# Weight loads, a norm block and four squares moved within the first phases of a fused three-layer block

## What is computed

```python
def gated_deltanet_mixer(h, w_in, conv_w, a_log, dt_bias, norm_w, w_out):
    proj = h @ w_in
    qkv, z, b_logit, a_logit = jnp.split(proj, [...], axis=-1)
    qkv = jax.nn.silu(causal_depthwise_conv(qkv, conv_w))
    q, k, v = jnp.split(qkv, [GDN_QK, 2 * GDN_QK], axis=-1)
    q, k = l2_normalize(q ...), l2_normalize(k ...)
    beta = jax.nn.sigmoid(b_logit)
    g = -jnp.exp(a_log) * jax.nn.softplus(a_logit + dt_bias)
    o = chunked_gated_delta_rule(q, k, v, g, beta)
    o = rms_norm(o, norm_w) * jax.nn.silu(z)
    return o @ w_out
```

## Time and profile before

| | us |
|---|---|
| median of 3 runs | 924.78 |
| lowest, highest | 924.2, 925.02 |
| the profiled execution | 924.2 |
| span of the profiled execution, first to last instruction | 922.2 |
| TensorE busy in it | 880.4 (95%) |
| VectorE busy | 693.7 (75%) |
| ScalarE busy | 509.7 (55%) |
| mean granted clock of TensorE | 0.974 of 2.4 GHz |

### The profile page before, as it was taken

The page is one execution under the profiler, slowest core; times in us unless marked ns, Lnnn a source line. Parts: engine busy times, 40 slices in busy tenths (PEclk is TensorE's granted clock), DMA queues, the critical chain, the costliest instruction groups (busy, mean ns, idle before and its releaser), DMA issues.

```text
span 922.2 us, 16363 instructions
## 1 busy us (share of the span) xinstructions
PE 880.4 (95%) x6434; PEld 820.2 (89%) x6434; DVE 693.7 (75%) x1116; ACT 509.7 (55%) x728; POOL 46.0 (5%) x48
## 2 busy tenths in 40 slices
PE   5899999989897999999999999999999989999997
PEld 5899998779776999999997899999887779999995
DVE  5677888945756777777758578899998789955874
ACT  5597877546445555555545564333345566445642
POOL 0001110122010000000000000000001220001000
PEclk9999999979998999999999979999999999999999
DMA  8735664620465477777776616555454445555441
GB/s 253 229 93 176 210 177 148 168 57 2 159 203 185 138 250 250 251 250 250 250 266 229 215 60 206 162 188 184 152 183 138 136 138 183 184 183 170 137 150 47
DMA packets 139476, 161.58 MB, mean 175 GB/s; under 512 B 17156, under 2 KB 112284, under 8 KB 139420
## 3 DMA queue, kind: packets, MB, share of 16 engines
q1 hardware_dynamic: 139419, 160.80, 53.6%
HBM read 156.58 MB, written 4.21 MB: 174 GB/s over the span
## 4 chain that ended last, share of the span: by engine, by line
PE 72%; DVE 15%; ACT 7%; issue 2%; DMA 2%; SPq 0%; DVEq 0%; ACTq 0%
PE psum L480 22%; PE psum L482 21%; PE psum L481 21%; DVE w_lo L1376 5%; PE psum L765 3%; DVE cv L1819 2%; ACT w_hi L933 2%; DMA w_raw<-in_sc_w_out_dram 1%; DVE Tq L1604 1%; DVE outer L1602 1%; DVE cacc L1525 1%; PE psum L635 1%; ACT junk L966 1%; DMA x<-in_x_dram 1%; PE psum L869 1%
## 5 line engine op out<-in xcount | busy, mean ns | idle before, releaser
L1376 DVE TENSOR_TENSOR w_lo<-w_raw,w_hi 128x1024 fp32r<-128x1024 f32 x264 | 321.0, 1239 | 139.2 <-ACT w_hi L933 138.1
L933 ACT ACTIVATE w_hi<-w_raw 128x1024 fp32r<-128x1024 f32 x264 | 274.1, 1057 | 213.2 <-PE psum L482 168.2
L480 PE MATMUL psum<-hT_hi,w_hi 128*128 128x256 f32 x1216 | 350.2, 288 | 6.3 <-DVE w_lo L1376 5.6
L481 PE MATMUL psum<-hT_lo,w_hi 128*128 128x256 f32 x1216 | 347.2, 286 | 0.0
L482 PE MATMUL psum<-hT_hi,w_lo 128*128 128x256 f32 x1216 | 347.2, 286 | 0.0
L480 PEld LDWEIGHTS psum<-hT_hi,w_hi 128*128 128x128 f32 x1216 | 236.9, 195 | 7.6 <-issue 4.4
L481 PEld LDWEIGHTS psum<-hT_lo,w_hi 128*128 128x128 f32 x1216 | 236.9, 195 | 0.3 <-issue 0.2
L482 PEld LDWEIGHTS psum<-hT_hi,w_lo 128*128 128x128 f32 x1216 | 236.6, 195 | 0.0
L1819 DVE SCALAR_TENSOR_TENSOR cv<-aP,par,cv 128x256 f32<-128x256 f32 x240 | 98.4, 477 | 0.0
L480 PE MATMUL psum<-w_hi,hT_hi 128*128 128x512 f32 x224 | 91.6, 409 | 4.1 <-DVE w_lo L1376 4.1
L482 PE MATMUL psum<-w_hi,hT_lo 128*128 128x512 f32 x224 | 87.5, 390 | 0.0
(11 more groups left out here) (283 smaller groups left out, 1059.1 us busy)
## 6 DMA issues: line engine op xcount, KB each, us to landing
w_raw<-in_w_in_dram SPq DMA_DIRECT2D x44, 1024.0 KB, 5.1
w_raw<-in_sc_w_in_dram SPq DMA_DIRECT2D x32, 1024.0 KB, 7.5
w_raw<-in_gdn_w_in_dram SPq DMA_DIRECT2D x24, 1024.0 KB, 5.5
ada<-in_w_ada_dram SPq DMA_DIRECT2D x24, 512.0 KB, 5.1
w_raw<-in_gdn_w_out_dram SPq DMA_DIRECT2D x8, 1024.0 KB, 5.3
w_raw<-in_sc_w_out_dram SPq DMA_DIRECT2D x8, 1024.0 KB, 7.5
w_raw<-in_w_ret_out_dram SPq DMA_DIRECT2D x8, 1024.0 KB, 4.9
w_raw<-in_w_conv_out_dram SPq DMA_DIRECT2D x4, 1024.0 KB, 4.9
```

The source lines that it names most:

```text
L480: pe.matmul(o, l_hi, r_hi, start=start, stop=False, skip_group_check=True)
L481: pe.matmul(o, l_hi, r_lo, start=False, stop=False, skip_group_check=True)
L933: act.activation(w_hi[j % 2 * 2 + h][:, :, :], raw[slot][:, h * KH2:(h + 1) * KH2, :], ACT.Copy).then_inc(hi_ready, 1)
L1376: return dve.tensor_tensor(o, whole, hi.bitcast(F32), ALU.subtract)
```

## The change

It has three parts. On SyncE, the loads of chunks 2 and 3 go behind the loads of `ba_raw` and the 14 small loads. On ScalarE, squares 4 and 5 leave the end of the qkv phase, and squares 4 to 7 stand in chunks 0 to 3 of z (before: 6 and 7 in chunks 0 and 1). On VectorE, the block of `bgt`, `ngk` and `wdec` at chunk 6 goes behind the two splits of its chunk, and its first wait asks for 1 of the two transposes instead of 2.

```diff
             chunk(0, 0, qkv_cols(0), wait=False)
             chunk(1, 1, qkv_cols(1), wait=False)
-            chunk(2, 2, qkv_cols(2), wait=False)
             ba0 = GQKV + GV
...
-            chunk(3, 3, qkv_cols(3), wait=False)
...
-            for g in range(RING, FIRST["gdn_out"]):
-                if g < FIRST["z"]:
+            for g in range(2, FIRST["gdn_out"]):
+                if g < 4:
+                    chunk(g, g, qkv_cols(g), wait=False)
+                elif g < FIRST["z"]:
                     chunk(g, g % RING, qkv_cols(g))
...
-            squares(4)
-            squares(5)
             silu(COUNT["qkv"] - 1)
 
             def beside_z(i, j, done):
                 c = 4 * i + j
-                if c < 2:
-                    squares(6 + c)
+                if c < 4:
+                    squares(4 + c)
...
             for c in range(COUNT["qkv"]):
-                if c == 6:
-                    dve.wait_ge(bg_turned, 2)
-                    dve.tensor_copy(bgt[:, :, :], bank(6, P)[:, 0:NT, :]).then_inc(bgt_ready, 1)
...
                 split_lo(0, 0, c + 1, 1)
                 split_lo(0, 0, c + 2, 0)
...
+                if c == 6:
+                    dve.wait_ge(bg_turned, 1)
+                    dve.tensor_copy(bgt[:, :, :], bank(6, P)[:, 0:NT, :]).then_inc(bgt_ready, 1)
+                    dve.wait_ge(bgt_ready, 1)
+                    dve.wait_ge(lnss_ready, 1)
...
```

More of the change, by code:

```diff
@@ L1580, in _ @@
                     dve.tensor_copy(par[:, 1:4, :].rearrange("p a n -> p (a n)")[:, 0:376], psum[:, 5, 0:376]).then_inc(small_ready, 1)
+                if c == 6:
[3 more added lines that the diff above has]
+                    dve.wait_ge(lnss_ready, 1)
+                    for t in range(NT):
+                        i = dve.scalar_tensor_tensor(out=twos(ngk[:, t, :]), in0=over(lnss[:, t, :], P, 2), scalar=-0.5,
+                                                     in1=twos(bgt[:, t, gr]), op0=ALU.mult, op1=ALU.subtract)
+                    i.then_inc(ngk_ready, 1)
+                    dve.wait_ge(ngk_ready, 1)
+                    dve.wait_ge(bg_turned, 2)
+                    dve.tensor_tensor(wdec[:, :], psum[:, 6, SEQ:SEQ + VH], ngk[:, 0, :], ALU.add).then_inc(wd_sub, 1)
                 if c in (8, 10, 12, 14):
```

## The result

| us | before | after |
|---|---|---|
| median | 924.33 (5 runs, 923.28 to 925.02) | 933.32 (5 runs, 931.78 to 934.69) |
| the profiled execution | 924.2 | 932.75 |
| its span | 922.2 | 930.7 |
| mean granted clock in it | 0.974 | 0.967 |

The ratio is 1.0098 with an interval from 1.0084 to 1.0111: 9.0 us slower, where 5.0 were forecast and the range ended at 932.4. Slower was right, the size was not.

A forecast was written before the change was run, and what follows sets the result against it. TensorE was taken as the bound. A 0, C 2.3, B 1.1 and one clock fall 1.6 made 5.0 us, added to the 924.78 us median for 929.8 us, with a range from 927.4 to 932.4.

The forecast's parts named there:

- Part A: SyncE's queue at the start: chunk 2 lands at about 23 us, early enough for TensorE, so the cost is 0.
- small-transfer rule: Start loads: transfers under 64 KB are descriptor-dominated; 14 small loads would take 9.5 us and cost TensorE about 3.4 us.
- Part C: VectorE at chunk 6: L635 waits 2.7 us for the moved block instead of 0.4, costing 2.3 us.
- Part B: ScalarE at the turn to z: L622 waits 2.9 us for square 4, less 1.8 of slack, net 1.1 us.
- The slack: z phase: TensorE's two waits for weight splits at 170 and 178 us fall away, giving back 1.8 us.
- The clock: Behind the two new waits: one fall to 1.2 GHz for 3.4 us, costing 1.6 us; chance 0.36.
- B's bounds: Cost at the turn to z: 0.6 us if a square comes earlier, 2.9 if VectorE's splits are held up.
- the case without a fall: Behind the two new waits the clock stays up, giving 928.2 us; chance 0.22.
- Rival 2: Both new waits, at L635 and L622, end in a clock fall, giving 931.4 us; chance 0.25.
- Rival 3: At the start chunk 2 lands after 25.5 us: up to 3.4 us more, 930 to 934 us; chance 0.06.
- rival 4: At the start x lands sooner, winning up to 1.9 us: 926.3 us (same, chance 0.06) or 922.9 (faster, 0.02).

The follow-up runs named there:

- A alone: Only the loads of chunks 2 and 3 moved behind the small loads, on the kernel before: median 925.38 us, ratio 0.9999 (0.9983 to 1.0015).
- With the filler: Kernel before with only the VectorE block moved, plus 20 useless matmuls ahead of L635: median 927.45 us, ratio 1.0034 (1.0016 to 1.0052).
- the run with its filler: Kernel before with only the squares moved, plus 21 useless matmuls ahead of L622: median 924.69 us, ratio 1.0000 (0.9985 to 1.0016).
- the whole change with the clock kept up: Changed kernel with useless matmuls in its two new waits, at L635 and L622: median 927.46 us, mean 927.40, ratio 1.0030 (1.0015 to 1.0046).
- best_fill2: Kernel before with fillers at `ba_lo` (18), last part of gdn_out (24), second norm (40, 22) and third norm (12): median 924.02 us, ratio 0.9997.

## Why the prediction was right in sign and short in size

**Part A, taken at 0.** The queue did what the steps say: the small loads went out earlier, chunk 2 was split at 23.58 us, and TensorE didn't wait at 28 us. The small loads were issued 4.5 us sooner and not 6.1 (17.98 us for 22.49), and chunk 2 then landed in under the forecast 6.5 us. The time agrees with 0 within its error (+0.9, error 0.7). What the steps left out is chunk 3: the prediction followed chunk 2 to its landing and put chunk 3 down as the next 1 MB. In the profile of A alone, and in one more, it landed late enough to push `ba_raw` back by 1.9 us. By two of five profiles A costs 1.9 us then and nothing otherwise; its mean share, 0.8 us, can't be told from 0 by the runs. The Trainium skill's small-transfer rule ("DMA: Bandwidth & Descriptors", section "Bandwidth"), which would have made A dear, isn't borne out: chunk 2 was issued directly behind the same 14 loads at 17.98 us and in ScalarE's hands at 23.58.

**Part C, taken at 2.3.** The wait was 2.65 us for a predicted 2.7, and the copies behind it lie 2.3 us later. This step was right. With the filler C keeps 3.3 us, with an error of 0.5.

**Part B, taken at 1.1.** The wait was 2.79 us for a predicted 2.9. The slack was under-sized: 1.8 us were taken from TensorE's idle time in the two waits, and the lag fell by 2.4 us. The waits as the matmuls' rows show them are not all of it: in the kernel before, the weight loads of TensorE wait 2.6 us in two waits in the same place, and the lag went down by about that. So B's own cost is about 0.4, not 1.1, as the run with its filler has it (error 0.6).

**The waits together.** 3.4 us were forecast for A, B and C together, and 3.5 were measured for the whole change with the clock kept up. The misses in the three are small and don't explain the 4 us.

**The clock, taken at 1.6: this step failed.** I allowed one fall of 3.4 us for the two waits, 1.6 us. Measured were 5.5 us (error 0.8) by the fillers, and 5.0 by the mean clock. It failed in two ways. First the length: "a fall has lasted 3.4 us where dense work follows" came from the two short stretches of the earlier trace rows, but the profile of before also has falls of 10.2 and 13.7 us, where the work is sparser. At L622 it was 6.8 us each time, and what follows the wait is eight matmuls of one column each in 1.84 us before the dense work begins. Whether these make the fall long was not tried, and behind the `ba_lo` wait it was 3.4 us in some profiles and 6.8 in others with the same work following. Second the number: the earlier trace rows gave one stretch of 2.4 us with a fall and one without, and I took one of two. In the four profiles with each new wait and no filler there, it fell at L622 in four (6.8 us each) and behind L635 in three (3.4 us each). By what these falls cost in the rows, 2.9 + 0.75 x 1.5 = 4.0 us are to be expected. With the 3.5 us of waits, which hold A's share, that makes 7.5 of the 9.0. The remaining 1.5 us lie within twice the error of the 5.5 (0.8) and stay open; the falls in other places, which also vary in length from profile to profile, could hold them.

**The range.** It was to take in both falls with B's bounds, but both falls with B at 2.9 give 924.8 + 2.3 + 2.9 + 3.2 = 933.2, and it ended at 932.4. That this sum comes near the measured 933.3 would have been luck: B costs 0.4 and not 2.9, and the clock 5.5 and not 3.2.

The Trainium skill ("TensorE: Matmul & The Clock Gate", section "Why this matters for your kernels") warns only of longer gaps than these. The rule was weighed as the case without a fall, 928.2 us; the traces disagree with it seven times in eight, and 928 is what the kernel takes only when fillers keep TensorE busy (927.4).

**The profiled pair misled a little.** Of the 8.5 us between the two profiled executions, 2.6 come from the `ba_lo` wait, which both kernels have. That it fell in one and not in the other is chance, and so is the missing fall behind L635. The two spans differ by 8.5 us and the means by 9.0, but one of the causes in the pair is not the change: the pair alone would have given a wrong list.

**Rivals.** Rival 2, both falls, was nearest in kind; it gave 931.4, since it priced each at 3.4 us of low clock. Rival 3 (chunk 2 late) and rival 4 (x sooner) didn't happen: the first table load stands 0.5 us later, not 1.9 sooner.

## What to carry to other kernels

Where TensorE is the bound, a new wait of 2 to 3 us in dense matmuls costs its length, less the slack behind it, and then a stretch at half clock, 3.4 to 6.8 us long here (1.5 to 3 us of time), so price both, and take the fall as the likely case. Before moving a producer behind other work of its engine, look whether its consumer's place moves with it: here TensorE's order stayed and both moves became waits. A wait that can't be removed can be filled with useless matmuls, counted so that they end just ahead of its end; a place that is off costs time instead, so read the wait's place from the trace, and judge the result by many runs.

## What the runs showed of the hardware

- The same wait of 2.4 us for `ba_lo` was followed by 1.2 GHz in six profiles and by 2.4 GHz in three (0.50 in that of after, 1.00 in that of before). Whether the clock falls behind a wait of 2.4 us is thus a matter of chance here, and one profile can't tell it.
- At L622 the stretch at 1.2 GHz was 6.8 us in all four profiles; behind L635, where dense matmuls follow at once, 3.4 us in three and none in one.
- The long stretch at 200 us, in the small matmuls of the solve, was 10.2 us in the profile of before and 17.1 us in that of after (0.50 over 200.5 to 217.0), with no change of code there; over the fourteen profiles it was 6.8 to 17.1 us. What sets it was not tried.
- The page shows a clock of 1.00 ahead of the first record, which need not be so: in the profile of after the first record begins at 19.5 us, and up to there the matmuls of 256 columns stand 0.21 us apart, from there on 0.12.
- The granted clock alone doesn't rank kernels: best_fill2 spent 36.0 us at 1.2 GHz against 50.0 of the kernel before, and was not faster.
